# Decay exponents with the triangle as weights and a 512-column moving side

## The chip, the core and the metric

The program runs on one core of a Trainium2 chip. The metric is the device time of one execution in microseconds. Before the change the median of three runs is 1035.26 us (1033.83 to 1036.64).

## The reference, cut to what matters

Two transformer-like blocks follow each other on 256 tokens of width 1024: a hybrid mixer (state-space part and short convolutions) with a mixture of 32 experts, and then a recurrent and linear-attention mixer with a dense feed-forward part. The change touches the state-space part alone. It has 16 heads, and its decay matrix is

```python
a_dt = dt * a                                   # one number for each token and head
ac = jnp.cumsum(a_dt, axis=2)
seg = ac[..., :, None] - ac[..., None, :]       # sum of a_dt over tokens s < k <= l
decay_in = jnp.exp(jnp.where(causal, seg, -jnp.inf))
y_diag = jnp.einsum("bcgls,bcgrls,bcsgrp->bclgrp", cb, decay_in, xdt)
```

The kernel computes it in two blocks of 128 tokens, not in the reference's chunks of 64. For a head and a block, the exponent for the pair (s, l) is the sum over tokens k of [k > s] * a_dt[k] * [k <= l]: a product of two 128x128 triangles with a_dt between them.

## The kernel before, in words

Each engine has its own instruction stream, written out by hand, and the streams meet only in counting semaphores. The input weights come in units of 2 MB into a ring of six slots on SyncE's queue, and are used in granules of 128x1024 numbers. For granule g ScalarE writes the rounded half w_hi (`hi`, L532), VectorE the remainder w_lo (`lo`, L542), both as fp32r and in two alternating buffers, and TensorE multiplies (`turn_gran`, L557: 24 matmuls of 256 columns). Granule g can only be split when g-2 has been used.

Granules 20 to 43 (G_SC to G_WO) are those of the short-convolution part. Between them TensorE does the state-space part: after every even granule from 20 to 34 comes `seg(it)` (L1744), the decay exponents of four heads, with it = 0 to 7 (block b = it // 4, four heads of 16 each time), and after every even granule from 22 on, behind the seg, `y_same(it - 1)` (L1757), the product of the masked decay with the inputs. The chain for one `it` is:

- GpSimd, `seg_left(it)` (L800): seg_l = m_gt times a_dt for four heads, 128x512. It waits until TensorE has done seg(it - 1), as there is one seg_l.
- TensorE, `seg(it)`: four matmuls, seg_l of a head as weights and the triangle m_le as moving side, all plain f32. It also waits until ScalarE has emptied bank 5.
- ScalarE, `exp_seg(it)` (L934): the exponential, from bank 5 to seg_e, after its `hi` of that granule.
- GpSimd, `mask_seg(it)` (L810): seg_e times the causal C.B product.
- TensorE, `y_same(it)`, which waits for seg_m.

GpSimd's order of work here is: dt (to dt_ready), seg_left(0), xdt for both blocks (L837), skip of x_tok(0) (L849), then for it = 1 to 8 seg_left(it), mask_seg(it - 1) and something more at some (x_tok(1) at 1, the decay of xdt at 5, gate_y at 7). VectorE's order is, for each granule: gate_sc (from granule 30), lo(g), conv_sc (granules 26 to 29: four small operations, two of them with two SBUF operands), keep_y (granules 25, 29, 33, 37: adds TensorE's y from bank 6 to x_tok). keep_y(n) waits for y_same(2n + 1), and what is behind it in VectorE's queue, the next lo among it, waits too.

The tile seg_l is also used, much earlier, for rows of small parameters (`prow`), and dt_t has a tile of its own. m_gt and m_le are the strict lower and the upper triangle of ones.

After granule 59 come routing and the experts, whose weights are loaded to ring slots as their granules are split.

Of the kernel before, what the change touches and what calls it, by code (L numbers as in the profile page):

```python
# [22 lines left out]
F32 = mybir.dt.float32  # L23
F32R = mybir.dt.float32r
I32 = mybir.dt.int32
ALU = mybir.AluOpType
# [3 lines left out]
P = 128  # L30
T = 256
TB = T // P
# [4 lines left out]
SSD_W, HEADS, HD, STATE, GROUPS = 1024, 16, 64, 128, 2  # L37
# [36 lines left out]
def bcast(ap, shape):  # L74
    return ap.broadcast_to(shape)
# [8 lines left out]
def build(nc, ctx, x, w, out):  # L84
    def sb(name, shape, dt=F32, where=ctx):
        return where.enter_context(nc.sbuf_tensor(name, shape, dt))

    def sem(name):
        return ctx.enter_context(nc.semaphore(name))
# [13 lines left out]
    res = sb("res", [P, TB, D])  # L103
    ident = sb("ident", [P, P])
    m_le = sb("m_le", [P, P])
    m_gt = sb("m_gt", [P, P])
    ones = sb("ones", [P, P])
    blk64 = sb("blk64", [P, P])
    iota_f = sb("iota_f", [P, P])
# [13 lines left out]
    bank = [ctx.enter_context(nc.psum_tensor(f"bank{i}", [P, 512], F32)) for i in range(8)]  # L123


    ph = ExitStack()
# [2 lines left out]
    z_tok = sb("z_tok", [P, TB, D], where=ph)  # L129
    bc_t = sb("bc_t", [P, 4, T], where=ph)  # L130
    cbm = sb("cbm", [P, GROUPS, 3, P], where=ph)
    seg_l = sb("seg_l", [P, 4, P], where=ph)
    seg_e = sb("seg_e", [P, 2, 4, P], where=ph)
    pad = sb("pad", [P, 3, T + 3], where=ph)
    cv = sb("cv", [P, 3, T], where=ph)
    prow = seg_l[:, 0:2, :]
    dt_t = sb("dt_t", [HEADS, T], where=ph)
    adt = sb("adt", [P, 8, TB, HEADS], where=ph)
    ef = sb("ef", [P, 2, HEADS], where=ph)
    ph.close()  # L140
    ph = ExitStack()
# [23 lines left out]
    ph = ExitStack()  # L165
# [12 lines left out]
    m_gtc = sb("m_gtc", [P, P], where=ph)  # L178
# [139 lines left out]
    dt_ready = sem("dt_ready")  # L318
# [3 lines left out]
    cb_ready = sem("cb_ready")  # L322
    xdt_ready = sem("xdt_ready")
    skip_ready = sem("skip_ready")
    seg_lhs = sem("seg_lhs")
    seg_raw = sem("seg_raw")
    seg_exp = sem("seg_exp")
    seg_m = sem("seg_m")
# [119 lines left out]
    link_dve, link_act, link_pool = counter(dve_chain), counter(act_chain), counter(pool_chain)  # L448
# [312 lines left out]
    @block.gpsimd  # L761
    def _(pool):
        def mask(tile, op, step, mult, base=0):
            link_pool(pool, nc.gpsimd.memset(tile, 1.0))
            link_pool(pool, nc.gpsimd.affine_select(out=tile, in_=tile, compare_op=op, fill=0.0, base=base,
                                                    pattern=[[step, P]], channel_multiplier=mult))
        nc.gpsimd.memset(neg_half, -0.5)
        mask(ident[:, :], ALU.is_equal, 1, -1)
# [20 lines left out]
        nc.gpsimd.tensor_scalar(adt[:, 0, :, :], adt[:, 0, :, :], -1.0, None, ALU.mult).then_inc(dt_ready, 1)  # L789


        def seg_left(it):

            b, q = divmod(it, 4)
            if it == 0:
                pool.wait_ge(dt_ready, 1)
                pool.wait_ge(par_turned, 2)
            else:
                pool.wait_ge(seg_raw, it)
            nc.gpsimd.tensor_tensor(seg_l[:, :, :], bcast(m_gt[:, :].unsqueeze(1), [P, 4, P]),  # L800
                                    bcast(adt[:, 0, b, 4 * q:4 * q + 4].unsqueeze(2), [P, 4, P]),
                                    ALU.mult).then_inc(seg_lhs, 1)

        def mask_seg(it):

# [25 lines left out]
            nc.gpsimd.tensor_tensor(sm[:, 32 + n:33 + n], sm[:, 28 + n:29 + n], neg_half[:, 0:1],  # L831
                                    ALU.pow).then_inc(ssd_rstd, 1)

        seg_left(0)
        pool.wait_ge(x_kept, KC)
        for b in range(TB):
            ins = nc.gpsimd.tensor_tensor(by_head(xdt, b), by_head(x_tok, b),  # L837
                                          bcast(adt[:, 7, b, :].unsqueeze(2), [P, HEADS, HD]), ALU.mult)
        ins.then_inc(xdt_ready, 1)
        for it in range(9):  # L840
            if 1 <= it < 8:
                seg_left(it)
            if it >= 1:
                mask_seg(it - 1)
            if it == 0:
                pool.wait_ge(xdt_ready, 1)
            if it < TB:
                v = by_head(x_tok, it)
                nc.gpsimd.tensor_tensor(v, v, bcast(bc16[:, 2, :].unsqueeze(2), [P, HEADS, HD]),  # L849
                                        ALU.mult).then_inc(skip_ready, 1)  # L850
            if it == 5:
                pool.wait_ge(y_raw, 4)
                pool.wait_ge(ef_ready, 1)
                nc.gpsimd.tensor_tensor(by_head(xdt, 0), by_head(xdt, 0),
                                        bcast(ef[:, 0, :].unsqueeze(2), [P, HEADS, HD]),
                                        ALU.mult).then_inc(xdt_decayed, 1)
            if it == 7:
                gate_y(0)
                gate_y(1)
# [20 lines left out]
        nc.gpsimd.memset(lru_w[:, :, :, :], 0.0).then_inc(const_ready, 1)  # L880
        link_pool(pool, nc.gpsimd.memset(lpad[:, :, 0:3], 0.0))
        link_pool(pool, nc.gpsimd.memset(z_t[:, :], 1.0))
        link_pool(pool, nc.gpsimd.tensor_tensor(m_gtc[:, :], m_gt[:, :], blk64[:, :], ALU.mult))
        nc.gpsimd.memset(sm[:, 64:65], 1.0).then_inc(const_ready, 1)
        pool.wait_ge(g_kept, 2)
        pool.wait_ge(ld_c, 16 * 5)
# [817 lines left out]
    def _(pe):  # L1704
# [17 lines left out]
        def ssd_start():  # L1722

            pe.wait_ge(dt_ready, 1)
            pe.wait_ge(const_ready, 2)
            nc.tensor.matmul(bank[7][:, 0:HEADS], m_gt[:, :], adt[:, 0, 0, :], start=True, stop=True)
            nc.tensor.matmul(bank[7][:, HEADS:2 * HEADS], m_le[:, :], adt[:, 0, 1, :], start=True, stop=True)\
              .then_inc(ef_raw, 1)
            pe.wait_ge(silu_done, XC)
            pe.wait_ge(x_kept, KC)  # L1730
            for g in range(GROUPS):
                nc.tensor.matmul(bank[5 + g][:, 0:T], bc_t[:, g, 0:P], bc_t[:, 2 + g, :], start=True, stop=True)
                nc.tensor.matmul(bank[5 + g][:, T:T + P], bc_t[:, g, P:T], bc_t[:, 2 + g, P:T], start=True,
                                 stop=True).then_inc(cb_raw, 1)

        def seg(it):

            pe.wait_ge(seg_lhs, it + 1)
            if it == 0:
                pe.wait_ge(cb_ready, GROUPS)  # L1740
            else:
                pe.wait_ge(seg_exp, it)
            for j in range(4):
                mm = nc.tensor.matmul(bank[5][:, j * P:(j + 1) * P], seg_l[:, j, :], m_le[:, :], start=True,  # L1744
                                      stop=True)
            mm.then_inc(seg_raw, 1)

        def y_same(it):
# [58 lines left out]
        for t in range(2):  # L1807
            pe.wait_ge(xbc_copied, 10 + 2 * t)
            for j in range(4):
                g = G_Z + 4 * t + j  # L1810
                flow_gran(pe, g, [bank[2 * t + b][:, :] for b in range(TB)], act_p, 2 * j)
                if g == G_Z + 1:
                    pe.wait_ge(dt_kept, 1)
                    for b in range(TB):
                        mm = nc.tensor.transpose(bank[6][:, b * HEADS:(b + 1) * HEADS],
                                                 dt_t[:, b * P:(b + 1) * P], ident[0:HEADS, 0:HEADS])
                    mm.then_inc(dt_raw, 1)
        ssd_start()
        for g in range(G_SC, G_WO):
            hf, j = divmod(g - G_SC, 12)  # L1820
# [40 lines left out]
        for c in range(KC + 2):  # L1861
            if c < KC:
                if c >= 4:
                    pe.wait_ge(*((tok_act, (c - 4) // 2 + 1) if c % 2 == 0 else (tok_dve, (c - 5) // 2 + 1)))
                for b in range(TB):
                    mm = nc.tensor.transpose(bank[c % 4][:, b * P:(b + 1) * P], tok[:, b, c * P:(c + 1) * P],
                                             ident[:, :])
                mm.then_inc(tok_turned, 1)
            if c >= 2:
                k = c - 2  # L1870
                pe.wait_ge(tok_act if k % 2 == 0 else tok_dve, k // 2 + 1)
                for b in range(TB):
                    mm = nc.tensor.matmul(bank[6 + b][:, 0:NG + NE], tok_t[:, k, b * P:(b + 1) * P],  # L1873
                                          w_rt[:, k, :], start=(k == 0), stop=(k == KC - 1))
# [5 lines left out]
        for o, last in ((NE, m_lt), (2 * NE, ones)):  # L1880
            nc.tensor.matmul(bank[5][:, o:o + NE], ones[:, :], rt[:, 4, 0, :], start=True, stop=False)
            mm = nc.tensor.matmul(bank[5][:, o:o + NE], last[:, :], rt[:, 4, 1, :], start=False, stop=True)
# [5 lines left out]
        with pe.Fori(0, n_rounds) as r:  # L1888
            with pe.Fori(0, NE // 8) as i:
                for s in range(2):  # L1890
# [3 lines left out]
                    for half in range(2):  # L1894
                        for c in range(4):
                            for b in range(TB):
                                o = (4 * half + c) * P
                                mm = nc.tensor.matmul(bank[5 + half][:, c * P:(c + 1) * P], tok[:, b, o:o + P],  # L1898
                                                      onehot[:, s, b, :], start=(b == 0), stop=(b == TB - 1))
# [187 lines left out]
```

## Time and profile before

| what | us |
|---|---|
| median of three runs | 1035.26 |
| lowest, highest | 1033.83, 1036.64 |
| the profiled execution's own time | 1035.04 |
| its span, first to last instruction | 1033.3 |
| TensorE matmuls busy | 795.7 (77%) |
| VectorE busy | 443.0 (43%) |
| ScalarE busy | 325.7 (32%) |
| GpSimd busy | 75.5 (7%) |
| mean granted TensorE clock, share of 2.4 GHz | 0.892 |

PE stands for TensorE, PEld for its weight loads, DVE for VectorE, ACT for ScalarE, POOL for GpSimd. A row of a timeline has the start, the duration (of a group: from the first start to the last end), engine, line, operation, output and inputs, shapes, the count, and in brackets how long the engine had stood before it and what released it. TensorE's matmuls are pipelined, so that the recorded durations overlap; their step is read from start to start. A plain f32 matmul appears as two records.

### The profile page before, as it was taken

Reading aid. Unit: us, or ns where it says so; the run is one execution under the profiler, and the core shown is the slowest. Engines: PE = TensorE matmul, PEld = TensorE weight load, DVE = VectorE, ACT = ScalarE, POOL = GpSimd, SP = SyncE. Lnnn points to the kernel's source line nnn. Section 1 sums busy time; section 2 is a strip of 40 time slices with the busy share of each in tenths; the row PEclk is TensorE's granted clock in tenths of the full one; section 3 lists DMA queues with packets and bytes.
Section 4 is the critical chain, followed back from the end, with each engine's and each line's share of the span. In section 5 each row is a group of like instructions: output and inputs, shape, how many; then the busy total and the mean of one; then the engine's idle time right before and its main releaser. Section 6 shows DMA issues by size and latency. Waiting matters only on the chain.

```text
span 1033.3 us, 16106 instructions
## 1 busy us (share of the span) xinstructions
PE 795.7 (77%) x6814; PEld 629.3 (61%) x6814; DVE 443.0 (43%) x754; ACT 325.7 (32%) x520; POOL 75.5 (7%) x100
## 2 busy tenths in 40 slices
PE   5999999985667466546557547576898979999996
PEld 4978998765424243322424214243887779999995
DVE  4855848554313031311213112134747655455554
ACT  4754345631010001001001000102485454444443
POOL 1008433100000000000000000000001000000000
PEclk9999999995969678886889778788999989999999
DMA  5895244356799999999899999999843544565101
GB/s 206 260 386 178 95 154 162 131 213 274 317 427 428 427 410 392 427 427 426 351 427 426 429 426 375 426 428 356 316 133 113 183 162 163 175 209 188 41 1 41
DMA packets 69735, 287.05 MB, mean 278 GB/s; under 512 B 11505, under 2 KB 34334, under 8 KB 57374
## 3 DMA queue, kind: packets, MB, share of 16 engines
q1 hardware_dynamic: 69346, 285.38, 70.3%
q8 instruction: 61, 1.00, 0.4%
q10 hardware_dynamic: 316, 0.58, 0.2%
q14 instruction: 12, 0.10, 0.0%
HBM read 284.90 MB, written 1.05 MB: 277 GB/s over the span
## 4 chain that ended last, share of the span: by engine, by line
PE 48%; issue 28%; DMA 14%; DVE 5%; ACT 3%; POOL 1%; ACTq 0%; POOLq 0%; SPq 0%; DVEq 0%
PE bank L557 13%; DMA down_a<-in_w_down_dram 13%; PE bank L1926 7%; PE bank L1913 7%; PE bank L591 5%; PE bank L1898 4%; PE bank L1939 4%; PE bank L569 3%; DMA ring<-in_w_in_dram 1%; DVE w_lo L542 1%; PE bank L1744 1%; ACT w_hi L532 1%; DVE h_m L1521 1%; PE bank L1757 1%; PE bank L1873 1%
## 5 line engine op out<-in xcount | busy, mean ns | idle before, releaser
L557 PE MATMUL bank<-act_p,w_hi 128*128 128x256 f32 x1440 | 268.3, 288 | 9.8 <-issue 5.8
L542 DVE TENSOR_TENSOR w_lo<-ring,w_hi 128x1024 fp32r<-128x1024 f32 x138 | 178.9, 1297 | 157.2 <-ACT w_hi L532 157.0
L557 PEld LDWEIGHTS bank<-act_p,w_hi 128*128 128x128 f32 x1440 | 227.9, 194 | 14.0 <-issue 9.2
L532 ACT ACTIVATE w_hi<-ring 128x1024 fp32r<-128x1024 f32 x138 | 145.9, 1058 | 195.8 <-PE bank L557 136.2
L557 PE MATMUL bank<-act_p,w_lo 128*128 128x256 f32 x720 | 205.5, 285 | 0.0
L557 PEld LDWEIGHTS bank<-act_p,w_lo 128*128 128x128 f32 x720 | 139.9, 194 | 0.0
L1529 DVE COPY y_e<-bank 32x256 f32<-32x256 f32 x64 | 27.2, 425 | 194.4 <-PE bank L1926 194.0
L1926 PE MATMUL bank<-down_b,h_t 128*32 128x256 f32 x512 | 48.4, 544 | 79.7 <-issue 74.0
L591 PE MATMUL bank<-w_hi,act_q 128*128 128x512 f32 x304 | 95.3, 394 | 0.4 <-issue 0.4
L1048 ACT ACTIVATE y_e<-bank 32x256 f32<-32x256 f32 x64 | 23.9, 373 | 218.3 <-PE bank L1926 217.9
L1913 PE MATMUL bank<-ring,x_t 128*32 128x256 f32 x1536 | 89.4, 385 | 0.0
L1926 PE MATMUL bank<-down_a,h_t 128*32 128x256 f32 x512 | 42.1, 485 | 56.7 <-DMA down_a<-in_w_down_dram 45.5
L1926 PEld LDWEIGHTS bank<-down_b,h_t 128*32 128x32 f32 x512 | 22.1, 149 | 102.9 <-issue 92.2
L1913 PEld LDWEIGHTS bank<-ring,x_t 128*32 128x32 f32 x1536 | 51.3, 112 | 33.5 <-issue 4.1
L1045 ACT ACTIVATE h_e<-bank 128x128 f32<-128x128 f32 x32 | 8.9, 277 | 197.5 <-PE bank L1913 197.5
L1926 PEld LDWEIGHTS bank<-down_a,h_t 128*32 128x32 f32 x512 | 18.6, 135 | 78.2 <-DMA down_a<-in_w_down_dram 48.9
L591 PEld LDWEIGHTS bank<-w_hi,act_q 128*128 128x128 f32 x304 | 55.5, 188 | 14.0 <-issue 1.9
L1898 PE MATMUL bank<-onehot,tok 128*128 128x128 f32 x256 | 41.1, 333 | 29.1 <-issue 24.5
L1898 PEld LDWEIGHTS bank<-onehot,tok 128*128 128x128 f32 x256 | 39.5, 244 | 34.3 <-issue 29.6
L591 PE MATMUL bank<-w_lo,act_q 128*128 128x512 f32 x152 | 59.4, 391 | 0.0
L569 PE MATMUL bank<-w_hi,act_p 128*128 128x512 f32 (+1 forms) x160 | 46.6, 376 | 2.5 <-DVE w_lo L542 2.4
L1521 DVE TENSOR_TENSOR h_m<-h_e,bank 128x128 f32<-128x128 f32 x32 | 11.9, 371 | 80.5 <-ACT h_e L1045 80.5
(330 smaller groups left out, 879.9 us busy)
## 6 DMA issues: line engine op xcount, KB each, us to landing
ring<-in_w_up_dram SPq DMA_DIRECT2D x24, 2048.0 KB, 21.7
ring<-in_w_gate_dram SPq DMA_DIRECT2D x24, 2048.0 KB, 17.3
ring<-in_w_in_dram SPq DMA_DIRECT2D x16, 2048.0 KB, 18.7
down_b<-in_w_down_dram SPq DMA_DIRECT2D x16, 2048.0 KB, 25.5
down_a<-in_w_down_dram SPq DMA_DIRECT2D x16, 2048.0 KB, 24.2
ring<-in_w_ffn_in_dram SPq DMA_DIRECT2D x22, 1024.0 KB, 6.6
pair_d<-in_w_gate_dram SPq DMA_DIRECT2D x8, 2048.0 KB, 26.8
pair_d<-in_w_up_dram SPq DMA_DIRECT2D x8, 2048.0 KB, 31.3
```

The lines of the kernel that those rows point to most:

```text
L532: nc.scalar.activation(parts(w_hi, g, view), view, ACT.Copy).then_inc(split_hi, 1)
L542: nc.vector.tensor_tensor(parts(w_lo, g, view), view, h, ALU.subtract).then_inc(split_lo, 1)
L557: mm = nc.tensor.matmul(dst, parts(wt, g, grans[g][1])[:, k, :], a[:, x_part, k, :], start=(k == 0 and i == 0), stop=(k == KC - 1 and i == 2))
L569: mm = nc.tensor.matmul(dsts[b], a[:, x_part, k0 + k, b * P:(b + 1) * P], parts(wt, g, grans[g][1])[:, k, :], start=(k0 + k == 0 and i == ...
L591: mm = nc.tensor.matmul(banks[2 * b + half][:, :], a_chunk[:, x_part, b * P:(b + 1) * P], wt[:, g % 2, half * 512:(half + 1) * 512], start ...
L1048: ins = nc.scalar.activation(y_e[CAP * e:CAP * (e + 1), 256 * j:256 * (j + 1)], bank[2][CAP * j:CAP * (j + 1), 0:256], ACT.Copy)
L1521: nc.vector.tensor_tensor(h_m[:, :].rearrange("p (c r) -> p r c", c=FF // P), h_e[:, :].rearrange("p (r c) -> p r c", c=FF // P), bank[0][ ...
L1529: ins = nc.vector.tensor_copy(y_e[CAP * e:CAP * (e + 1), 256 * j:256 * (j + 1)], bank[2][CAP * j:CAP * (j + 1), 0:256])
L1898: mm = nc.tensor.matmul(bank[5 + half][:, c * P:(c + 1) * P], tok[:, b, o:o + P], onehot[:, s, b, :], start=(b == 0), stop=(b == TB - 1))
L1913: mm = nc.tensor.matmul(bank[0][CAP * j:CAP * (j + 1), 0:2 * P], x_t[:, s, c, CAP * e:CAP * (e + 1)], gu[:, :, c, j * P:(j + 1) * P], star ...
L1926: mm = nc.tensor.matmul(bank[2][CAP * j:CAP * (j + 1), 0:256], h_t[:, CAP * c:CAP * (c + 1)], dn[:, c, 256 * j:256 * (j + 1)], start=(c == ...
L1939: nc.tensor.matmul(bank[M_BANK[q]][:, :], gmat[:, b * P:(b + 1) * P], y_e[:, half * 512:(half + 1) * 512], start=True, stop=True)\
```

## The change

The roles are swapped: m_gt is now the weights of every matmul, and the moving side is m_le times a_dt, for four heads side by side in 512 columns. All of it is fp32r, a form with fewer mantissa bits; so a_dt is split once into a rounded part and a remainder (`split_adt`), the moving side is built twice (`seg_right`), and the two matmuls accumulate in bank 5. dt_t and prow move into seg_e.

```diff
-    m_gt = sb("m_gt", [P, P])
+    m_gt = sb("m_gt", [P, P], F32R)
-    seg_l = sb("seg_l", [P, 4, P], where=ph)
+    seg_r = sb("seg_r", [P, 2, 4, P], F32R, where=ph)
-    prow = seg_l[:, 0:2, :]
-    dt_t = sb("dt_t", [HEADS, T], where=ph)
+    prow = seg_e[:, 0, 0:2, :]
+    dt_t = seg_e[0:HEADS, 1, 0:2, :].rearrange("p h l -> p (h l)")
+    adt_r = sb("adt_r", [P, 2, TB, HEADS], F32R, where=ph)
...
-        def seg_left(it):
+        def split_adt():
+
+            pool.wait_ge(dt_ready, 1)
+            link_pool(pool, nc.gpsimd.tensor_copy(adt_r[:, 0, :, :], adt[:, 0, :, :]))
+            link_pool(pool, nc.gpsimd.tensor_tensor(adt_r[:, 1, :, :], adt[:, 0, :, :],
+                                                    adt_r[:, 0, :, :].bitcast(F32), ALU.subtract))
+
+        def seg_right(it):
 
             b, q = divmod(it, 4)
             if it == 0:
-                pool.wait_ge(dt_ready, 1)
                 pool.wait_ge(par_turned, 2)
             else:
                 pool.wait_ge(seg_raw, it)
-            nc.gpsimd.tensor_tensor(seg_l[:, :, :], bcast(m_gt[:, :].unsqueeze(1), [P, 4, P]),
-                                    bcast(adt[:, 0, b, 4 * q:4 * q + 4].unsqueeze(2), [P, 4, P]),
-                                    ALU.mult).then_inc(seg_lhs, 1)
+            for n in range(2):
+                ins = nc.gpsimd.tensor_tensor(
+                    seg_r[:, n, :, :], bcast(m_le[:, :].unsqueeze(1), [P, 4, P]),
+                    bcast(adt_r[:, n, b, 4 * q:4 * q + 4].bitcast(F32).unsqueeze(2), [P, 4, P]), ALU.mult)
+            ins.then_inc(seg_rhs, 1)
...
-        seg_left(0)
+        split_adt()
+        seg_right(0)
...
-                seg_left(it)
+                seg_right(it)
...
-            pe.wait_ge(seg_lhs, it + 1)
+            pe.wait_ge(seg_rhs, it + 1)
...
-            for j in range(4):
-                mm = nc.tensor.matmul(bank[5][:, j * P:(j + 1) * P], seg_l[:, j, :], m_le[:, :], start=True,
-                                      stop=True)
+            for n in range(2):
+                mm = nc.tensor.matmul(bank[5][:, :], m_gt[:, :],
+                                      seg_r[:, n, :, :].rearrange("p h l -> p (h l)"), start=(n == 0), stop=(n == 1))
             mm.then_inc(seg_raw, 1)
```

The masks are now written by `mask` through a plain view of an fp32r tile, and two other uses of m_gt read it through a bitcast.

## Rows read from the trace of the kernel before

**Rows 1.** The page: the chain that ended last, by engine.
```profile
PE 48%; issue 28%; DMA 14%; DVE 5%; ACT 3%; POOL 1%; ACTq 0%; POOLq 0%; SPq 0%; DVEq 0%
```
**Rows 2.** Busy time by stretch: us, each engine's busy (count), PEclk, DMA, GB/s.
```profile
89.00:152.00 63.00, 62.72 (x523) 62.03 (x522) 38.16 (x39) 24.92 (x37) 33.49 (x21) 1.00 0.37 134
...
177.00:178.00 1.00, 1.00 (x7) 1.00 (x6) 1.00 (x1) 0.18 (x1) 0.00 (x0) 0.50 0.88 377
...
400.00:500.00 100.00, 52.58 (x590) 27.85 (x581) 19.04 (x45) 8.70 (x20) 0.00 (x0) 0.78 1.01 427
```
**Rows 3.** Timeline of PE: segs 0 to 2, y_same(0), first matmuls of granules 28, 30.
```profile
89.16 1.05 PE L1744 MATMUL bank<-m_le,seg_l 128*128 128x128 f32 x8
...
96.31 1.05 PE L1744 MATMUL bank<-m_le,seg_l 128*128 128x128 f32 x8
97.20 1.00 PE L1757 MATMUL bank<-xdt,seg_e 128*128 128x64 f32 x8
98.02 0.48 PE L557 MATMUL bank<-act_p,w_hi 128*128 128x256 f32 x2
...
103.86 1.05 PE L1744 MATMUL bank<-m_le,seg_l 128*128 128x128 f32 x8
...
116.21 0.47 PE L557 MATMUL bank<-act_p,w_hi 128*128 128x256 f32 x2
...
123.96 0.48 PE L557 MATMUL bank<-act_p,w_hi 128*128 128x256 f32 x2
```
**Rows 4.** Timeline of POOL, 84 to 115 us.
```profile
84.08 0.30 POOL L789 TENSOR_SCALAR adt<-adt 128x32 f32<-128x32 f32 x1
84.46 1.04 POOL L800 TENSOR_TENSOR seg_l<-m_gt,adt 128x512 f32<-128x512 f32 x1
85.46 4.75 POOL L837 TENSOR_TENSOR xdt<-x_tok,adt 128x1024 f32<-128x1024 f32 x2
90.28 1.91 POOL L849 TENSOR_TENSOR x_tok<-x_tok,bc 128x1024 f32<-128x1024 f32 x1
92.15 2.02 POOL L800 TENSOR_TENSOR seg_l<-m_gt,adt 128x512 f32<-128x512 f32 x1
94.13 1.29 POOL L810 TENSOR_TENSOR seg_e<-seg_e,cbm 128x512 f32<-128x512 f32 x1
...
104.99 1.04 POOL L800 TENSOR_TENSOR seg_l<-m_gt,adt 128x512 f32<-128x512 f32 x1 [3.49 <-PE bank L1744]
...
113.55 1.48 POOL L810 TENSOR_TENSOR seg_e<-seg_e,cbm 128x512 f32<-128x512 f32 x1
```
**Rows 5.** Timeline of DVE, 84 to 124 us.
```profile
84.52 2.06 DVE L542 TENSOR_TENSOR w_lo<-ring,w_hi 128x1024 fp32r<-128x1024 f32 x1 [1.36 <-ACT w_hi L532]
...
90.45 2.82 DVE L542 TENSOR_TENSOR w_lo<-ring,w_hi 128x1024 fp32r<-128x1024 f32 x1 [2.68 <-ACT w_hi L532]
...
102.27 1.23 DVE L542 TENSOR_TENSOR w_lo<-ring,w_hi 128x1024 fp32r<-128x1024 f32 x1 [2.92 <-ACT w_hi L532]
...
112.03 1.84 DVE L1309 SCALAR_TENSOR_TENSOR sc_f<-pad,par,sc_f 128x256 f32<-128x256 f32 x2
113.80 2.31 DVE L542 TENSOR_TENSOR w_lo<-ring,w_hi 128x1024 fp32r<-128x1024 f32 x1
...
122.47 1.38 DVE L542 TENSOR_TENSOR w_lo<-ring,w_hi 128x1024 fp32r<-128x1024 f32 x1
```
**Rows 6.** Timeline of PE: matmuls of 512 columns with fp32r operands.
```profile
181.18 0.62 PE L591 MATMUL bank<-w_hi,act_q 128*128 128x512 f32 x2
...
181.85 0.62 PE L591 MATMUL bank<-w_hi,act_q 128*128 128x512 f32 x2
```
**Rows 7.** Timeline of ACT: the rounded half of granule 23.
```profile
93.12 1.06 ACT L532 ACTIVATE w_hi<-ring 128x1024 fp32r<-128x1024 f32 x1 [1.95 <-PE bank L557]
```
**Rows 8.** The chain in order of time: start, us, what, and the records merged.
```profile
171.52 2.52 issue
174.04 4.51 PE bank L557 x24
```

More of the change, by code:

```diff
@@ L324, in build @@
     skip_ready = sem("skip_ready")
-    seg_lhs = sem("seg_lhs")
+    seg_rhs = sem("seg_rhs")
     seg_raw = sem("seg_raw")
@@ L763, in mask @@
         def mask(tile, op, step, mult, base=0):
-            link_pool(pool, nc.gpsimd.memset(tile, 1.0))
-            link_pool(pool, nc.gpsimd.affine_select(out=tile, in_=tile, compare_op=op, fill=0.0, base=base,
+            plain = tile.bitcast(F32)
+            link_pool(pool, nc.gpsimd.memset(plain, 1.0))
+            link_pool(pool, nc.gpsimd.affine_select(out=tile, in_=plain, compare_op=op, fill=0.0, base=base,
                                                     pattern=[[step, P]], channel_multiplier=mult))
@@ L882, in _ @@
         link_pool(pool, nc.gpsimd.memset(z_t[:, :], 1.0))
-        link_pool(pool, nc.gpsimd.tensor_tensor(m_gtc[:, :], m_gt[:, :], blk64[:, :], ALU.mult))
+        link_pool(pool, nc.gpsimd.tensor_tensor(m_gtc[:, :], m_gt[:, :].bitcast(F32), blk64[:, :], ALU.mult))
         nc.gpsimd.memset(sm[:, 64:65], 1.0).then_inc(const_ready, 1)
@@ L1725, in ssd_start @@
             pe.wait_ge(const_ready, 2)
-            nc.tensor.matmul(bank[7][:, 0:HEADS], m_gt[:, :], adt[:, 0, 0, :], start=True, stop=True)
+            nc.tensor.matmul(bank[7][:, 0:HEADS], m_gt[:, :].bitcast(F32), adt[:, 0, 0, :], start=True, stop=True)
             nc.tensor.matmul(bank[7][:, HEADS:2 * HEADS], m_le[:, :], adt[:, 0, 1, :], start=True, stop=True)\
```

## The prediction

> **What bounds the kernel now.** I read the page first. The chain that ended last is TensorE for 48% and waiting with no recorded releaser for 28% [rows 1]; so a microsecond saved on TensorE counts only where TensorE is the one that is late. The state-space stage is such a place: from 89 to 152 us TensorE is busy 62.72 of 63 us at the full clock, VectorE 38.2 and GpSimd 33.5 [rows 2]. The chain in that stretch repeats one pattern: granule matmuls (L557), the decay exponents (L1744, 96.31 to 97.20: 0.89 us), y_same (L1757, to 98.02), two more granules [rows 3]. What ends at 152 us is passed on whole: the granules after it are in TensorE's order, the ring slots of the expert weights come free as granules are split, and the expert stage then runs at 427 GB/s with the DMA engines full [rows 2], from transfers that were started by then. I count a shift at 152 us one to one.
>
> Then I looked at how close the other engines are in that stretch, on the timelines of TensorE, GpSimd, VectorE and ScalarE. GpSimd works from 84.1 us on without a gap; the first mask (L810) ends at 95.42 and y_same(0) starts at 97.20: 1.8 us of slack, and the second seg_l ends at 94.17 against seg(1) at 96.31, 2.1 us [rows 3, 4]. Later GpSimd has gaps. VectorE is late at two places already: w_lo for granule 28 ends at 116.11 and the granule starts at 116.21; w_lo for granule 30 ends at 123.85 and the granule starts at 123.96 [rows 3, 5].
>
> One more thing is to be seen there: VectorE's operations on two SBUF tiles and GpSimd's do not overlap, they take turns. A w_lo takes 1.23 us alone, but 2.82 from 90.45, when GpSimd's x_tok multiply runs until 92.19: 1.08 us are left after that. The seg_l queued at 92.15 then ends at 94.17, 0.90 us after w_lo's end, and takes 2.02 us instead of 1.04 [rows 4, 5]. The one from 113.80 ends 1.08 us after the mask's end at 115.03. Whoever asked first goes first, for one instruction. Operations with one PSUM operand I take as not taking part. The Trainium skill has this as a rule (SBUF — State Buffer, Who interferes with whom): a VectorE instruction with two SBUF inputs and a GpSimd one that reads SBUF hold one port in turn. By that rule, the trace agrees; it speaks against this change, since whoever counts busy shares alone would find room for the added GpSimd work and get the 3.5 us gain of the third rival below.
>
> **The change part by part.**
> TensorE, removed: 4 f32 matmuls per step, recorded as 8 pieces, 0.89 us. Added: 2 fp32r matmuls of 512 columns. L591 has that form and runs three in 0.67 us (starts 181.18 and 181.85), 0.225 each [rows 6]; so 0.45 per step, a saving of 0.44, for 8 steps 3.5 us. The weights don't bind: they load beside the 512 columns as at L591. The Trainium skill (TensorE: Matmul & The Clock Gate, Back-to-back issue gap) gives about 131 ns sustained for 512 columns; by it the saving would be 0.63 per step. I go by the row.
> GpSimd, added: a second 128x512 multiply per step, 1.04 us alone, 1.0 from start to start, 0.90 when it comes right after a block (row at 92.15); 8 of them. The fp32r output is not seen on GpSimd in this trace: nearest are the f32 form (1.04) and the mask form (1.3), on VectorE the fp32r w_lo at its plain rate; I take 1.04, with 1.3 as the upper end (0 to 0.3 us more per operation), nothing below. Also added once: a copy and a subtract of 128x32 with their chain waits, 0.38 each by the step from 84.08 to 84.46 [rows 4], together 0.7 (0.2 to 1.4 if VectorE's turn falls between). The masks made as fp32r, the bitcasts and the moved tiles (prow and dt_t into seg_e) cost nothing: GpSimd makes the masks long before its work of 84 us, in a stand, and dt_t is read by TensorE before seg_e is first written, in the order of the code. DMA issues are the same ones, and no queue gets another wait; behind seg_right on GpSimd stand the masks, x_tok and xdt multiplies, and for them TensorE waits in order.
>
> **Start-up, replayed with the turns.** GpSimd after dt_ready at 84.4: split 0.7, a VectorE turn (w_lo 21) of 1.0, two multiplies to 88.1. seg(0) on TensorE is at 89.16: covered by 1.0. It ends 0.44 early, and granule 21 too (done 92.65). xdt twice (1.87 each): 91.85. w_lo(22), asked at 90.45, runs to 92.93, so granule 22 starts at 93.03 (before 93.37). x_tok to 94.7. ScalarE's split of 23 follows the end of granule 21 (before 93.12 to 94.18 [rows 7], now 92.7 to 93.7); so w_lo(23), which asked just after the first mask had begun, now asks at 93.8, long before it, and takes a turn to 95.8. (x_tok's 1.87 is the step from 90.28 to 92.15.) The two multiplies of seg_right(1) end at 97.7 and seg(1) runs 97.8 to 98.25, where TensorE came at 96.0. w_lo(24), asked at 97.4, takes the turn at 97.7 to 98.8, the mask ends at 99.9, y_same(0) at 100.8 against 98.02. So TensorE lags by 2.8 us there, after standing 1.8 and 1.75 us with 0.45 us of work between. Lower end: none of the two VectorE turns falls in, the mask ends at 95.42 + 2.7 = 98.1, and the lag is 1.0. x_tok, seg_right(2) and mask(1) end by 105.1, before seg(2) at 106.6.
>
> **The steps 2 to 4.** Count from seg(2)'s start S (before 103.86). GpSimd starts 1.13 later before (104.99), now 0.69. Multiplies to S+2.73; w_lo(26), held by keep_y, asks at S+2.1, gets S+2.73 to 3.81, then mask to 4.96; then VectorE's convolution pieces (0.42, 0.35, two of 0.5; the two took 1.84 from 112.03 when seg_l fell between) and w_lo(27) to S+7.1. seg(3) starts at S+7.04, its two multiplies and the mask alternate with convolution pieces 1 and 2: the mask ends at S+11.7, w_lo(28) at S+12.8. TensorE would want granule 28 at S+11.2. Before it started at S+12.35: so here 0.55 is lost, in place of 0.88 gained by two shorter steps. From granule 28 to 30 it was 7.75; now the second multiply and the mask end at 7.4 after granule 28's start, and w_lo(30) at 8.5: 8.6, a loss of 0.85 (if w_lo(30) gets its turn before the mask, 7.6: a gain of 0.1). After that VectorE has 1 us or more of slack before granule 34 and has no convolution piece beside seg(6) and seg(7), and the steps 5, 6 and 7 give 1.32 back.
>
> Sum: 2.8 - 0.1 + 0.55 + 0.85 - 1.3 = +2.8 us. With the low ends: 1.0 - 0.1 + 0.55 - 0.1 - 1.3 = 0.
>
> **The clock.** TensorE stood from 171.5 to 174.0 (2.52 us), and then, from 177 to 178, the granted clock is 0.50, 1.2 GHz [rows 2]. The 24 matmuls of the granule behind the stand have 4.51 us in the chain [rows 8]; two granules take 5.84 at the full clock (98.02 to 103.86 [rows 3]), so one 2.92, and 0.2 of the 4.51 is the end of the last matmul: 1.4 lost. The start-up lag puts 3.6 us of standing into 4.0 us, more than the first case, so I take the 1.4 as likelier than not. The Trainium skill (TensorE: Matmul & The Clock Gate, What's actually happening) says that activity is what releases the throttle; nothing above needs it.
>
> The profiled execution took 1035.04 us with a span of 1033.3; the median is 1035.26, 0.2 above. 1035.04 + 2.8 + 1.4 + 0.1 (half of that difference) = 1039.3.
>
> **Rivals and chances.** What a measurement of this kernel tells from no change is 0.3%, 3.1 us.
> 1. Forecast: GpSimd start-up makes TensorE wait, VectorE's turns cost steps 3 and 4, the clock drops once. 1039.3, own range 1038 to 1041.5. 45%.
> 2. The same without the drop (the short seg between the two waits, or a shorter stand): 1037.8, or 1036.9 with the kinder turn at granule 30. 25%.
> 3. The added GpSimd work is hidden in its later gaps, the start-up slack of 1.8 us nearly holds, and the 3.5 us on TensorE arrive: 1031.6. For it: GpSimd stands 3.49 us before the seg_l of 104.99 [rows 4], and each mask is then ready early. Against it: in start-up it stands nowhere, and 0.7 + 2.0 us are more than 1.8 even before any turn. 12%.
> 4. A draw: the low ends, or the clock drop avoided and other turns luckier, 1034.5 to 1036.5. 18%.
> The slower side is the first two: steps 2 to 7 sum to nothing (-0.1 + 0.55 + 0.85 - 1.3), so the lag at y_same(0) and the clock are the result, and from 3.1 us of both together it can be told from no change. Faster by over 0.3%: 0.10 (from 3). Slower: 0.40 from 1 and 0.08 from 2, 0.48. Same: 0.42. Range 1033.2 to 1041.7; it takes in 1, 2 and 4 with 0.3 us per operation more on fp32r, and leaves out 3 and a tail. The likeliest's own range is 1038 to 1041.5.
>
> **What would show it.** Right: on GpSimd two multiplies back to back of 1.04 alone; L1744 at 0.45 per step; TensorE idle before seg(1) and before y_same(0), 2.5 to 4 us together, released by GpSimd; a stretch of clock 0.50 around 100 to 104; w_lo(28) and w_lo(30) longer than 2 us, with TensorE idle before those granules by over 1 us. Wrong: seg(1) and y_same(0) without a wait, and y_same(7) ending before 152.2; or fp32r matmuls that cost as much as the four f32 ones; or the lag at 152 us vanishing by the last expert.

## The result, and the profile after

The changed kernel takes 1030.59 us (median of 14 runs, 1028.59 to 1033.63) where the kernel before takes 1036.14 (14 runs): ratio 0.9949, 95% interval 0.994 to 0.9959. It is 5.5 us faster. I had forecast 1039.3, slower, with a range of 1033.2 to 1041.7; the result lies below it.

The page after, first the engines and later the instruction queue and the chain:

```profile
span 1029.7 us, 16020 instructions
...
PE 795.6 (77%) x6766; PEld 627.8 (61%) x6766; DVE 442.2 (43%) x754; ACT 326.1 (32%) x520; POOL 87.2 (8%) x110
...
q8 instruction: 60, 0.98, 0.4%
...
PE 44%; issue 27%; DMA 16%; DVE 5%; ACT 3%; POOL 2%; SPq 1%; ACTq 0%; POOLq 0%; DVEq 0%
```

TensorE has 48 matmuls and 48 weight loads fewer (it had 6814 of each): 96 instructions. GpSimd has 11.7 us more to do.

**The stage of the change is slower, as forecast.** Timeline of TensorE in the changed kernel, the lines that answer to [rows 3]; L1755 is the decay exponents, L1768 y_same, L558 a granule; the last line is the first matmul behind y_same(7):

```profile
89.63 0.63 PE L1755 MATMUL bank<-seg_r,m_gt 128*128 128x512 f32 x2
...
98.04 0.72 PE L1755 MATMUL bank<-seg_r,m_gt 128*128 128x512 f32 x2 [1.60 <-POOL seg_r L809]
100.24 1.97 PE L1768 MATMUL bank<-xdt,seg_e 128*128 128x64 f32 x8 [1.48 <-POOL seg_e L820]
101.97 0.77 PE L558 MATMUL bank<-act_p,w_hi 128*128 128x256 f32 x2
...
109.95 0.62 PE L1755 MATMUL bank<-seg_r,m_gt 128*128 128x512 f32 x2
...
122.68 0.47 PE L558 MATMUL bank<-act_p,w_hi 128*128 128x256 f32 x2 [1.27 <-issue]
...
130.08 0.47 PE L558 MATMUL bank<-act_p,w_hi 128*128 128x256 f32 x2
...
156.82 0.48 PE L558 MATMUL bank<-act_p,w_hi 128*128 128x256 f32 x2
```

The granule behind y_same(0) starts at 101.97, where it was 98.02 [rows 3]; TensorE stood 1.60 and 1.48 us for GpSimd. The same stretch on GpSimd and VectorE, against [rows 4, 5]:

```profile
84.91 0.21 POOL L797 CAST adt_r<-adt 128x32 fp32r<-128x32 f32 x1
85.21 1.11 POOL L798 TENSOR_TENSOR adt_r<-adt,adt_r 128x32 fp32r<-128x32 f32 x1
86.39 2.04 POOL L809 TENSOR_TENSOR seg_r<-m_le,adt_r 128x512 fp32r<-128x512 f32 x2
88.39 3.77 POOL L848 TENSOR_TENSOR xdt<-x_tok,adt 128x1024 f32<-128x1024 f32 x2
92.24 2.77 POOL L860 TENSOR_TENSOR x_tok<-x_tok,bc 128x1024 f32<-128x1024 f32 x1
94.97 3.02 POOL L809 TENSOR_TENSOR seg_r<-m_le,adt_r 128x512 fp32r<-128x512 f32 x2
97.95 2.24 POOL L820 TENSOR_TENSOR seg_e<-seg_e,cbm 128x512 f32<-128x512 f32 x1
```

```profile
94.26 1.83 DVE L543 TENSOR_TENSOR w_lo<-ring,w_hi 128x1024 fp32r<-128x1024 f32 x1 [1.01 <-ACT w_hi L533]
97.69 1.37 DVE L543 TENSOR_TENSOR w_lo<-ring,w_hi 128x1024 fp32r<-128x1024 f32 x1 [1.61 <-ACT w_hi L533]
...
118.02 2.32 DVE L1320 SCALAR_TENSOR_TENSOR sc_f<-pad,par,sc_f 128x256 f32<-128x256 f32 x2
120.27 2.31 DVE L543 TENSOR_TENSOR w_lo<-ring,w_hi 128x1024 fp32r<-128x1024 f32 x1
...
128.77 1.21 DVE L543 TENSOR_TENSOR w_lo<-ring,w_hi 128x1024 fp32r<-128x1024 f32 x1
```

The two multiplies with an fp32r output take 2.04 us undisturbed, 1.0 each. VectorE's w_lo takes two turns between 94 and 99 us, and the first mask ends at 100.19 instead of 95.42. By stretch (us, busy of PE, PEld, DVE, ACT, POOL with counts, granted clock, DMA share, GB/s):

```profile
101.00:103.00 2.00, 2.00 (x11) 2.00 (x11) 0.00 (x0) 0.00 (x0) 2.00 (x2) 0.50 1.02 418
102.00:106.00 4.00, 4.00 (x21) 4.00 (x21) 0.00 (x0) 0.00 (x0) 3.28 (x4) 0.50 0.29 118
105.00:109.00 4.00, 4.00 (x29) 4.00 (x29) 0.64 (x1) 1.33 (x2) 0.28 (x1) 0.77 0.02 4
107.00:109.00 2.00, 2.00 (x19) 2.00 (x19) 0.64 (x1) 1.33 (x2) 0.00 (x0) 1.00 0.04 8
...
260.00:700.00 440.00, 273.66 (x3288) 156.61 (x3292) 101.77 (x260) 41.02 (x99) 0.00 (x0) 0.82 0.98 416
```

After the two stands the granted clock is 0.50, 1.2 GHz; from 107 us on it is 1.00 again. In the kernel before, the first matmul behind y_same(7) is

```profile
152.02 0.48 PE L557 MATMUL bank<-act_p,w_hi 128*128 128x256 f32 x2
```

The changed kernel is there at 156.82: 4.8 us late, of which 0.46 come from before the stage (its first matmul, the one with adt and m_gt, is at 84.89, before at 84.43). The stage itself takes 4.34 us more.

**The gain is in the expert stage, which the change does not touch.** SyncE's issues at the start and the end of that stage, before:

```profile
253.84 0.33 SPq L699 DMA_DIRECT2D down_a<-in_w_down_dram  x1
...
733.11 1.34 SPq L753 DMA_DIRECT2D lru_w<-in_lru_wa_dram  x2
```

and after:

```profile
258.57 0.33 SPq L700 DMA_DIRECT2D down_a<-in_w_down_dram  x1
...
727.76 1.34 SPq L754 DMA_DIRECT2D lru_w<-in_lru_wa_dram  x2
```

The stage begins 4.73 us later and ends 5.35 us earlier: 479.3 us have become 469.2. (Behind it these two executions lose 1.5 us of the difference over two granules, 786.03 to 795.88 us against 791.34 to 799.70: the same stand of 1.91 us is in front of it in both, and the clock behind it is 0.57 in the one and 1.00 in the other. So their spans differ by 3.6 us only.)

The code of the stage is the same, and so are its loads. It is a loop: eight groups of four experts, two groups in each pass, so that it jumps back three times. TensorE's timeline at the first matmuls behind each jump (L1898, in the changed kernel L1909); before:

```profile
371.87 1.86 PE L1898 MATMUL bank<-onehot,tok 128*128 128x128 f32 x7 [4.64 <-issue]
377.35 5.70 PE L1898 MATMUL bank<-onehot,tok 128*128 128x128 f32 x25 [3.62 <-issue]
...
494.66 1.04 PE L1898 MATMUL bank<-onehot,tok 128*128 128x128 f32 x7 [3.80 <-issue]
500.18 5.70 PE L1898 MATMUL bank<-onehot,tok 128*128 128x128 f32 x25 [4.48 <-issue]
...
616.96 1.04 PE L1898 MATMUL bank<-onehot,tok 128*128 128x128 f32 x7 [3.28 <-issue]
622.72 4.49 PE L1898 MATMUL bank<-onehot,tok 128*128 128x128 f32 x25 [4.71 <-issue]
```

and after:

```profile
375.98 5.46 PE L1909 MATMUL bank<-onehot,tok 128*128 128x128 f32 x32 [4.60 <-issue]
...
495.29 5.46 PE L1909 MATMUL bank<-onehot,tok 128*128 128x128 f32 x32 [4.68 <-issue]
...
614.39 5.95 PE L1909 MATMUL bank<-onehot,tok 128*128 128x128 f32 x32 [4.76 <-issue]
```

Both kernels stand at the jump, and the profile shows nothing that they wait for ("issue"). The kernel before stands a second time, after exactly 7 recorded matmuls; 3.62 + 4.48 + 4.71 = 12.8 us in all. The changed kernel doesn't. Its first waits are somewhat longer (14.0 us against 11.7), so that all waits together are 14.0 us against 24.5: 10.5 us less, and the stage is 10.1 us shorter. In the groups that follow without a jump (310.08 and 429.51 before, 312.23 and 431.76 after) there is no wait in either. That speaks for a wait that hangs on the place in the code, and not on data. The Trainium skill (Runtime: NRT & Kernel Launch, Instruction fetch mechanics) says that each engine's sequencer fetches its code by its own DMA queue in blocks of 256 instructions, that TensorE's instruction memory has room for 2048, and that a taken jump to code that is not at hand makes the engine wait for the fetch. The experiments ask whether that is it.

Why 10 us of TensorE's waiting count in a stage in which the DMA engines are nearly always full is seen in the stretches around the first two jumps (columns as above), before:

```profile
365.00:400.00 35.00, 23.51 (x280) 15.62 (x282) 9.85 (x25) 2.05 (x6) 0.00 (x0) 0.80 0.93 387
488.00:518.00 30.00, 19.01 (x200) 12.51 (x198) 8.18 (x21) 1.30 (x4) 0.00 (x0) 0.81 0.87 358
```

and after:

```profile
365.00:400.00 35.00, 25.61 (x318) 15.74 (x310) 11.16 (x28) 4.36 (x10) 0.00 (x0) 0.93 1.01 426
488.00:518.00 30.00, 22.09 (x289) 14.21 (x291) 10.15 (x25) 2.08 (x7) 0.00 (x0) 0.94 1.01 423
```

With two waits at a jump the transfers fall to 387 and 358 GB/s, with one they stay at 426 and 423 (at the third jump, from 612 to 640 us, it is 376 and 410). An expert's weights can only be overwritten when TensorE has used them, so a stand that is long enough should leave the queue with nothing to start; that it is this, and no other wait, is argued from the code, not tested by itself.

### The profile page after: what moved, and what is told of

Same layout as the page of the kernel before. It is cut to its first block, busy times and chain, and to the rows that moved or that the text cites. A ratio compares the mean times of both kernels' runs of the same rounds, so it can differ in the third digit from the quotient of the medians.

```text
span 1029.7 us, 16020 instructions
## 1 busy us (share of the span) xinstructions
PE 795.6 (77%) x6766; PEld 627.8 (61%) x6766; DVE 442.2 (43%) x754; ACT 326.1 (32%) x520; POOL 87.2 (8%) x110
## 4 chain that ended last, share of the span: by engine, by line
PE 44%; issue 27%; DMA 16%; DVE 5%; ACT 3%; POOL 2%; SPq 1%; ACTq 0%; POOLq 0%; DVEq 0%
DMA down_a<-in_w_down_dram 14%; PE bank L558 10%; PE bank L1937 7%; PE bank L1924 7%; PE bank L592 5%; PE bank L1909 4%; PE bank L1950 3%; PE bank L570 3%; DMA ring<-in_w_in_dram 2%; PE bank L1768 1%; DVE h_m L1532 1%; ACT w_hi L533 1%; DVE w_lo L543 1%; PE bank L1884 1%; DVE h_t L1537 1%
## 5 line engine op out<-in xcount | busy, mean ns | idle before, releaser
L558 PE MATMUL bank<-act_p,w_hi 128*128 128x256 f32 x1440 | 272.6, 291 | 11.5 <-issue 7.0
L558 PEld LDWEIGHTS bank<-act_p,w_hi 128*128 128x128 f32 x1440 | 231.9, 198 | 15.8 <-issue 10.4
L558 PE MATMUL bank<-act_p,w_lo 128*128 128x256 f32 x720 | 207.2, 288 | 0.0
L558 PEld LDWEIGHTS bank<-act_p,w_lo 128*128 128x128 f32 x720 | 142.0, 197 | 0.0
L1909 PE MATMUL bank<-onehot,tok 128*128 128x128 f32 x256 | 37.5, 317 | 18.6 <-issue 14.0
L1909 PEld LDWEIGHTS bank<-onehot,tok 128*128 128x128 f32 x256 | 36.7, 231 | 23.1 <-issue 18.4
```

The lines of the kernel that those rows point to most:

```text
L558: mm = nc.tensor.matmul(dst, parts(wt, g, grans[g][1])[:, k, :], a[:, x_part, k, :], start=(k == 0 and i == 0), stop=(k == KC - 1 and i == 2))
```

## The experiments

In all of them the time of the kernel before is measured beside. Places are counted in TensorE's instructions; the head is the first instruction of the expert loop, and a boundary is where one block of code ends and the next begins. A second wait after 7 recorded matmuls and their 7 weight loads puts a boundary 14 instructions behind the head of the kernel before; the changed kernel has 96 instructions fewer ahead of the loop, so there it is 110. A tiny f32 matmul is recorded as two matmuls and two weight loads, so it moves what is behind it by 4. The count can be read on the page: with 24 tiny matmuls the changed kernel has 6814 matmul records again.

The padding, here for 6, stands in TensorE's first stand, while it waits for the parameter rows:

```diff
+        pe.wait_ge(const_ready, 1)
+        for _ in range(6):
+            nc.tensor.matmul(bank[3][0:16, 0:16], ident[0:16, 0:16], ident[0:16, 0:16], start=True, stop=True)
         pe.wait_ge(ld_par, 16 * N_ROWS_A)
-        pe.wait_ge(const_ready, 1)
```

**1. The kernel before, 24 instructions added at the start.**

> The kernel before, with 6 tiny f32 matmuls (24 instructions) at TensorE's start, while it waits for the parameter rows; nothing else is changed. Theory P (place of the loop's head): in the kernel before, TensorE stands a second time after 7 recorded matmuls of L1898 at each of the three jumps back of the expert loop (3.62, 4.48, 4.71 us), since the rest of its code is not loaded yet; 24 instructions more ahead of the loop move the head over that boundary, the second waits vanish, and about 10 of the 12.8 us arrive: about 1026 us. Theory T (timing: the later arrival or another phase of the transfers made the second waits vanish): the start is not delayed, so the waits stay and the time is 1036 within 1 us.

Measured: 1021.48 us against 1036.05, ratio 0.9853 (0.9834 to 0.9872). More than expected: not only the second waits are gone, the first ones are too. Its timeline at a jump, and the instruction queue from 255 to 700 us (packets, MB, share):

```profile
367.08 3.73 PE L1900 MATMUL bank<-onehot,tok 128*128 128x128 f32 x32
```

```profile
q8 instruction: 7, 0.11, 0.1%
```

In the kernel before, and in the changed one, the same stretch has:

```profile
q8 instruction: 33, 0.54, 0.5%
```

33 packets of 16 KB (0.54 MB in 33) have become 7. The rival by timing has fallen: work added, nothing taken away, 14.6 us faster. The 32 first matmuls now take 3.73 us behind a jump too, where 25 of them took 5.70 behind the second wait: the granted clock is 1.00 from 366 to 371 us, and in the kernel before it is 0.50 from 371 to 383.

**2. The same padding behind the expert loop.**

```diff
+        for _ in range(6):
+            nc.tensor.matmul(bank[4][0:16, 0:16], ident[0:16, 0:16], ident[0:16, 0:16], start=True, stop=True)
         turn_pe(pe, 2, 1, nrm)
```

> A control: the kernel before with the same 6 tiny matmuls, but behind the expert loop. Theory P: the loop's head has not moved; the three second waits stay, 1036 within 1 us. If the added matmuls or the total length of the program mattered, and not what stands ahead of the loop, it would be as fast as the run with them at the start.

Measured: 1036.38 us, ratio 1.0004 (0.9992 to 1.0016), with all six waits. Only what stands ahead of the loop counts.

**3. The kernel before, 8 instructions at the start** (`range(2)` in the padding).

> The kernel before with 2 tiny f32 matmuls (8 instructions) at TensorE's start: the loop's head is still ahead of the boundary, by 6 instructions instead of 14. Theory P: the second wait is still there at each of the three jumps, now after 3 recorded matmuls instead of 7, and the time is 1036 to 1037 us. If any instructions at the start would do (a warmer start, another phase), it would be near 1021.5 us.

Measured: 1036.26 us, ratio 1.0003 (0.9988 to 1.0018). The second wait has moved by exactly 4 matmul records:

```profile
371.04 0.59 PE L1900 MATMUL bank<-onehot,tok 128*128 128x128 f32 x3 [4.73 <-issue]
376.28 6.07 PE L1900 MATMUL bank<-onehot,tok 128*128 128x128 f32 x29 [4.65 <-issue]
```

**4. The changed kernel, 96 instructions at the start** (`range(24)`).

> The changed kernel, with 24 tiny f32 matmuls (96 instructions, as many as the change took away from TensorE) at TensorE's start. Theory P: the expert loop's head is where it was before, the second waits after 7 matmuls of L1898 are back, 3 of some 4.3 us, and what is left is the change itself: the 4.3 to 4.8 us that TensorE lags at 152 us, so about 1040 to 1041 us. Theory T: the lag at the start of the expert stage is as in the changed kernel, so no second waits, 1030.6 within 1 us.

Measured: 1038.47 us, ratio 1.0017 (1.0001 to 1.0033). The second waits are back after 7 records, and the gain is gone with them; the profiled execution:

```profile
375.33 1.86 PE L1911 MATMUL bank<-onehot,tok 128*128 128x128 f32 x7 [4.89 <-issue]
380.94 5.44 PE L1911 MATMUL bank<-onehot,tok 128*128 128x128 f32 x25 [3.76 <-issue]
```

So the 96 instructions are what decided: with the loop in its old place the change makes the kernel slower, by 2.4 us (0.1 to 3.4). That is less than the 4 to 5 us that I expected.

**5. The changed kernel, 60 instructions at the start** (`range(15)`).

> The changed kernel with 15 tiny f32 matmuls (60 instructions) at TensorE's start: the loop's head is 50 instructions ahead of the boundary, between the changed kernel (110) and the kernel before (14). Theory P with a block that takes some 4.6 us to come: one wait of 4.6 us at each jump as in the changed kernel, and after 25 recorded matmuls of L1909 (4.3 us at 0.17 each) a second one of 0 to 1 us; the time is 1030.6 to 1033 us. If the second wait were all or nothing by some other rule, it would be 3.6 to 4.7 us and the time about 1038.5.

Measured: 1030.58 us, ratio 0.9945 (0.9926 to 0.9965).

```profile
375.16 4.68 PE L1911 MATMUL bank<-onehot,tok 128*128 128x128 f32 x25 [4.57 <-issue]
380.92 0.94 PE L1911 MATMUL bank<-onehot,tok 128*128 128x128 f32 x7 [1.08 <-issue]
```

The boundary is where the count puts it (14 + 96 - 60 = 50 instructions, 25 matmul records), and the second wait is short, 0.61 to 1.11 us at the three jumps. It is not the block's 4.6 us less the work ahead of the boundary, as I had it: that work alone takes 4.68. What stays nearly the same is the time from the first matmul behind the jump to the first one behind the boundary: 5.8 us here (375.16 to 380.92), 5.2 to 5.8 in experiment 3 with 3 records between, 5.5 to 5.8 in the kernel before with 7. The six waits are 17.3 us against 14.0 in the changed kernel; at the 14.6 us of time for 24.5 us of waiting of experiment 1 the added 3.3 would be worth 2 us, an estimate, and the time cannot tell that, as its interval is 2 us to either side.

**6. The kernel before, 72 instructions at the start** (`range(18)`).

> The kernel before with 18 tiny f32 matmuls (72 instructions) at TensorE's start: the head is 58 instructions behind the boundary instead of 10. If the loop's code then still covers as few blocks as in before_24_early: no waits, 1021.5 us within 1.5. If it reaches into one block more: a wait of some 4.6 us at each jump and one only, 1028 to 1032 us. Either outcome bounds the length of the loop's code.

Measured: 1022.65 us against 1036.29, ratio 0.987 (0.9848 to 0.9893). By its time this is my first outcome, by its waits neither: one jump of the three has a wait (4.99 us before 607.04), the others have none, and the instruction queue has 15 packets. That the loop's code just about fits into what stays loaded, and only when its head is near the start of a block, is my reading of 33, 7 and 15 packets; no run shows the room itself. Why it fits at two jumps and not at the third I have not settled.

**7. The changed kernel, 120 instructions at the start** (`range(30)`): the head stands as in experiment 1.

> The changed kernel with 30 tiny f32 matmuls (120 instructions) at TensorE's start, so that the loop's head stands where it does in before_24_early (10 instructions behind the boundary). Theory P with all of the loop then staying loaded: no wait before L1898 at any of the three jumps; the time is that of before_24_early plus what TensorE lags at 152 us through the change, 1021.5 + 4.3 = about 1025.8 us. If the change itself were faster and the place only noise: under 1021.5.

Measured: 1025.47 us against 1037.04, ratio 0.9897 (0.9876 to 0.9919); no wait at any jump, 7 packets. The change alone, at equal place, costs 4.0 us over experiment 1 (1025.47 - 1021.48, on different chips; by the ratios 0.0044 of 1036, 4.6 us). Both intervals together leave some 1.5 to 7.5 us, an estimate; with the 2.4 of experiment 4 the sign is clear, the size is not.

**8. GpSimd's part alone**, in the kernel of experiment 1:

```diff
+            nc.gpsimd.tensor_tensor(seg_x[:, :, :], bcast(m_gt[:, :].unsqueeze(1), [P, 4, P]),
+                                    bcast(adt_r[:, 1, b, 4 * q:4 * q + 4].bitcast(F32).unsqueeze(2), [P, 4, P]),
+                                    ALU.mult)
             nc.gpsimd.tensor_tensor(seg_l[:, :, :], bcast(m_gt[:, :].unsqueeze(1), [P, 4, P]),
```

> before_24_early with GpSimd's part of the change alone: the split of a_dt and a second 128x512 multiply in each step, into a tile that nobody reads (dt_t moved into seg_e as in the change, to make room). TensorE's matmuls as before. If the doubling on GpSimd is the cost: TensorE stands before seg(1) and y_same(0), the clock drops, and the time is 1021.5 + 4.3 + 3.5 = about 1029 us. If GpSimd has room for it: 1021.5 within 1 us.

Measured: 1027.69 us, ratio 0.9903 (0.9878 to 0.9927), 6.2 us over experiment 1. TensorE stands 1.60 us before seg(1) and 1.04 before y_same(0), and the granule behind starts at 102.32. So the added work on GpSimd (the split and the second multiply) is the cost, and the 3.5 us on TensorE are not enough to pay for it.

**9. One term alone.** The `range(2)` of seg_right and of seg are `range(1)`, `stop` is set at the first matmul, and 136 instructions are padded.

> The changed kernel with the first term alone: one multiply on GpSimd and one 512-column matmul per step (the remainder of a_dt is left out of the decay exponents), and 136 instructions at the start, head as in before_24_early. TensorE's part without GpSimd's doubling: 8 x (0.89 - 0.225) = 5.3 us less than before_24_early, less 0 to 1.5 us for the split on GpSimd: 1016.5 to 1018 us. If GpSimd's second multiply were harmless, this would be only 8 x 0.225 = 1.8 us faster than after_120_early.

Measured: 1022.24 us, ratio 0.9861 (0.9843 to 0.9879). My 1016.5 to 1018 is missed: it is 3.2 us better than experiment 7, so GpSimd's second multiply is not harmless (that would have been 1.8), but no better than the kernel before at the same place. Its timeline says why:

```profile
97.40 1.10 PE L1770 MATMUL bank<-xdt,seg_e 128*128 128x64 f32 x8 [1.27 <-POOL seg_e L820]
...
116.05 0.48 PE L558 MATMUL bank<-act_p,w_hi 128*128 128x256 f32 x2 [0.51 <-issue]
...
125.33 0.47 PE L558 MATMUL bank<-act_p,w_hi 128*128 128x256 f32 x2 [2.19 <-issue]
```

The 5.3 us saved on TensorE turn into waits of 1.27 for GpSimd and 0.16, 0.51 and 2.19 us for w_lo, which takes turns with GpSimd there (2.33, 2.32 and 1.99 us long, alone 1.22); and from 126 to 130 us the granted clock is 0.57. Here TensorE's own work is no longer what bounds the stage.

**10 and 11. GpSimd's order in start-up.** The skip multiplies come one step later:

```diff
-            if it < TB:
-                v = by_head(x_tok, it)
+            if 1 <= it <= TB:
+                v = by_head(x_tok, it - 1)
```

> The changed kernel with the skip multiplies of GpSimd (L860) one step later each, so that seg_right(1) and mask_seg(0) come right behind xdt. Number of TensorE's instructions as in the changed kernel. If the start-up on GpSimd is what makes TensorE stand (1.60 and 1.48 us) and the clock drop: no wait before seg(1) of over 0.7 us and none before y_same(0), clock 1.00 from 97 to 110 us, TensorE at y_same(7) some 4 to 5 us earlier, and 1026 us, as a shift there is passed on one to one. If the shift is swallowed by the expert stage: 1030 to 1031.

> The changed kernel with the later skip multiplies on GpSimd and 120 instructions at TensorE's start. Both gains together, if they are separate: after_120_early less 5.5 us, about 1020 us, some 1 to 2 us below before_24_early, as the two granule waits on VectorE (1.3 to 1.6 us) eat part of the 3.5 us on TensorE.

Measured: 1024.92 us, ratio 0.9893 (0.9873 to 0.9912), 5.7 us below the changed kernel; and with 120 instructions more 1021.89, ratio 0.9853 (0.9834 to 0.9871), 3.6 below experiment 7. In the first, the stand before seg(1) is gone, the one before y_same(0) is 0.52 us, the clock from 95 to 110 us is 1.00, and the granule behind y_same(7) starts at 150.77 instead of 156.82. I had expected no stand at all before y_same(0), and 1026 us. The forecast of 1020 for the second was 2 us too low. It beats both kernels, but not experiment 1, which has the old form of the exponents: same ratio.

**The stage by itself.** From the first matmul of the state-space stage (adt, m_gt) to the first one behind y_same(7), in the profiled executions:

| run | from, to | us |
|---|---|---|
| before | 84.43, 152.02 | 67.59 |
| before_24_early | 84.80, 152.40 | 67.60 |
| after | 84.89, 156.82 | 71.93 |
| after_96_early | 85.43, 156.86 | 71.43 |
| after_60_early | 85.67, 156.12 | 70.45 |
| after_120_early | 84.93, 155.41 | 70.48 |
| before_gpsimd_twice | 85.24, 159.51 | 74.27 |
| after_one_term | 85.02, 152.90 | 67.88 |
| after_reordered | 84.10, 150.77 | 66.67 |
| after_reordered_120 | 85.23, 151.89 | 66.66 |

In the other three runs, all with the old form, it is 67.59 or 67.60 too. This measures the change without the expert stage. As written the change costs 2.9 to 4.3 us, least in the two executions in which the low clock was shorter (0.59 and 0.71 from 102 to 106 us, 0.50 in the other two). With GpSimd's order changed it gains 0.9 us. A gain of that size does not show in the medians.

## Why the prediction was wrong

- **What failed** is the step "What ends at 152 us is passed on whole ... I count a shift at 152 us one to one". The shift was passed on to the start of the expert stage (4.73 us at 258.57), but that stage was not the same after: 96 instructions ahead of its loop were gone, the loop's head stood 110 instead of 14 instructions ahead of a block boundary, and three waits of TensorE of 12.8 us went (10.5 us net of the longer first waits). The stage became 10.1 us shorter. Experiment 4 shows it: with the 96 instructions back, the waits are back and the gain is gone. The trace before the change had the rows for it, but the share on the page did not: of the 28% "issue" in the chain 196.4 us are one piece at its end, from 830.96 us on, and the six waits at the jumps are 24.5. I named the 28% and asked nowhere what it is made of. No rival of mine had the place of code in it.
- **The local sum came out, in part by luck.** Forecast +4.2 us for the stage (2.8 and 1.4 for the clock), measured 4.34 in the profiled execution, and 2.9 to 3.8 in the other three with the same stage. The 4.34 are 2.6 of lag at y_same(0), 3.0 for the clock and -1.3 for steps 2 to 7, where I had 2.8, 1.4 and 0: two errors of 1.6 and 1.3 us cancel. At equal place of the loop it is 4.0 us in the medians (experiment 7 against 1).
- **Start-up**: forecast 2.8 us of lag at y_same(0) with stands of 1.8 and 1.75; measured 2.6 (start at 100.24 for 97.20, less the 0.46) with stands of 1.60 and 1.48. Experiments 8, 10 and 11 show that GpSimd's added work causes them.
- **The clock**: the drop came, from y_same(0) on. Its price was more than the 1.4: the 48 matmuls behind took 7.98 us (101.97 to 109.95) for 5.84, 2.1, and y_same(0) itself 1.73 for 0.82, 0.9 more. That it would come was less safe than it looks: the stand of 2.5 us from which I took the 1.4 was itself followed by a low clock in only six of the 13 profiled executions.
- **Steps 3 and 4**: granule 28 waited 1.27 us for w_lo, as worked out (w_lo and the convolution pieces 2.31 and 2.32 us long). At granule 30 w_lo got its turn before the mask (128.77, 1.21 us), the kinder of the two outcomes: 7.40 us from granule 28 to 30 (122.68 to 130.08) and not 8.6, against 7.75 before. A loss of 0.85 became a gain of 0.35, and that made up for most of the clock. The 1.32 that the later steps were to give back is what they gave.
- **TensorE's saving** of 0.44 per step: the two matmuls take 0.46 from start to the next (89.63 to 90.09), as forecast. The fp32r output costs GpSimd nothing (two multiplies 2.04 us).
- **Rival 3**, the only one on the faster side, gave 1031.6 and so nearly the time, but for a reason that did not happen: GpSimd's work was not hidden.

## What to carry to other kernels

An edit that changes how many instructions stand ahead of a loop moves the loop against the boundaries of its code blocks. Before a small difference in time is put down to the edit, compare the stages that it does not touch; where "issue" waits of 3 to 5 us stand behind a loop's jump, shift the loop by some instructions and measure again. And a busy share leaves out turns: 33 of 63 us on GpSimd looked like room, and there was none at the start of the stage, where the added work had to be done in order; moving the skip multiplies behind it (experiments 10 and 11) gave the loss back.

## What the runs showed of the hardware

- At a jump back TensorE stood 3.3 to 5.0 us for its code. With a boundary soon behind the head it stood a second time, until 5.2 to 5.9 us behind the first matmul: 4.65 to 4.75 us with 3 records between, 3.6 to 4.7 with 7, 0.6 to 1.1 with 25. With the head 10 instructions behind a boundary no wait was left, and the instruction queue moved 7 packets in place of 33.
- The Trainium skill (Runtime: NRT & Kernel Launch, Instruction fetch mechanics) has the blocks of 16 KiB and the wait at a jump, and the trace agrees (16 KB a packet, and the stands); it calls the cost of crossing a block's boundary mostly hidden, and soon behind a jump the second waits show that it was not. How far the boundaries lie from each other no run here measures.
- All six waits together were 24.5 us, and their removal gave 14.6: from 260 to 700 us the transfers went from 408 GB/s to 419, and from 262 to 700 us TensorE's waits before the down projection went from 119.5 us to 137.4.
- Stands of 1.60 and 1.48 us with 0.5 us of matmuls between them, and one of 2.19 us, were each followed by a granted clock near 0.5. But a stand alone does not decide it: the one of 2.5 us before the granule at 174.04 is in all 13 profiled executions, and behind it the clock fell to 0.50 to 0.53 over two microseconds in six of them, the kernel before among them, and stayed at 1.00 in seven. From the first matmul behind y_same(7) to the expert loop's first it is 103.0 to 103.4 us in the six and 101.8 to 102.1 in the seven: the low clock there costs some 1.3 us, and no edit of the runs goes with it.
